# Side matmuls of an attention loop placed in three groups per step instead of one

## The reference, cut to what matters

```python
p = split_in(h @ w_in)                    # one projection feeds everything below
y_a = mlstm_branch(...)                   # "ml":  mLSTM, then @ ml_w_o
y_b = mla_branch(...)                     # "mla": 8 heads, softmax attention, then @ mla_w_o
y_c = natten_branch(...)                  # "na":  8 heads, windowed attention with bias, then @ na_w_o
# attend: s = q @ k^T * scale; p = softmax(s); o = p @ v
y = (sigmoid(g_a) * y_a + sigmoid(g_b) * y_b + sigmoid(g_c) * y_c) @ w_out
```

## Time and profile before

| | |
|---|---|
| median of 3 runs | 2104.02 us (2099.68 to 2108.57) |
| the profiled execution | 2104.02 us, of which the span is 2102.2 us |
| mean granted TensorE clock | 0.903 |
| PE busy | 1733.3 us, 82% of the span |
| DVE, ACT, POOL busy | 51%, 35%, 30% |
| first S to last S of the loops na0, mla0, na1, mla1 (starts) | 388.9 to 507.6; 634.0 to 751.7; 1573.9 to 1643.5; 1737.9 to 1806.0 |

### The profile page before, as it was taken

How to read it: one execution, slowest core, us unless ns; L and a number is a source line. 1 busy time by engine, 2 the same in 40 slices (tenths; PEclk the granted TensorE clock), 3 DMA queues, 4 the chain that set the end, 5 groups by cost and what they waited for, 6 DMA issues and landing times.

```text
span 2102.2 us, 24715 instructions
## 1 busy us (share of the span) xinstructions
PE 1733.3 (82%) x9538; PEld 1456.1 (69%) x9538; DVE 1069.2 (51%) x1895; ACT 729.7 (35%) x1354; POOL 627.1 (30%) x380
## 2 busy tenths in 40 slices
PE   2594768999769998888989897676599869878998
PEld 1483548877457777656868686465598748778998
DVE  6786953143173335156746454426325265555555
ACT  3223324343333423242313131433334344435443
POOL 0441114222122212243535442430331311233443
PEclk9697879999779999988999998798899979998999
DMA  7342212211111123213443333220222202343553
GB/s 273 122 184 100 100 31 76 63 63 42 46 40 52 46 101 110 100 51 128 170 152 140 149 131 140 100 86 0 71 79 62 95 28 91 132 170 102 184 187 130
DMA packets 55846, 216.98 MB, mean 103 GB/s; under 512 B 17313, under 2 KB 17459, under 8 KB 41139
## 3 DMA queue, kind: packets, MB, share of 16 engines
q1 hardware_dynamic: 41232, 202.13, 27.2%
q10 hardware_dynamic: 14499, 13.29, 2.0%
HBM read 210.15 MB, written 5.24 MB: 102 GB/s over the span
## 4 chain that ended last, share of the span: by engine, by line
PE 66%; DVE 17%; ACT 5%; issue 4%; POOL 3%; DMA 3%; ACTq 1%; POOLq 0%; SPq 0%; DVEq 0%
PE bank L1494 35%; PE bank L1536 8%; PE bank L1508 6%; PE bank L1656 3%; PE bank L1769 3%; PE bank L1748 3%; PE bank L1518 2%; DVE mjunk L1002 2%; DVE acc L1002 2%; DVE arena L1028 2%; ACT wH L642 2%; POOL wL L511 2%; PE bank L1755 1%; DMA raw<-in_p_ff 1%; POOL wL L513 1%
## 5 line engine op out<-in xcount | busy, mean ns | idle before, releaser
L642 ACT ACTIVATE wH<-raw 128x1280 fp32r<-128x1280 f32 (+5 forms) x380 | 295.3, 833 | 661.3 <-PE bank L1494 410.2
L513 POOL TENSOR_TENSOR wL<-raw,wH 128x768 fp32r<-128x768 f32 (+5 forms) x190 | 325.4, 1717 | 477.7 <-ACT wH L642 460.4
L511 POOL TENSOR_TENSOR wL<-raw,wH 128x1280 fp32r<-128x1280 f32 (+5 forms) x98 | 231.3, 2360 | 682.4 <-ACT wH L642 682.4
L1494 PE MATMUL bank<-hH,wH 128*128 128x512 f32 (+1 forms) x976 | 349.6, 358 | 81.2 <-POOL hL L530 50.1
L1494 PE MATMUL bank<-hL,wH 128*128 128x512 f32 (+1 forms) x976 | 342.5, 351 | 0.0
L1494 PE MATMUL bank<-hH,wL 128*128 128x512 f32 (+1 forms) x976 | 342.1, 350 | 0.0
L1494 PEld LDWEIGHTS bank<-hH,wH 128*128 128x128 f32 x976 | 193.1, 198 | 121.1 <-issue 54.7
L1494 PE MATMUL bank<-oH,wH 128*128 128x512 f32 (+1 forms) x576 | 198.3, 344 | 35.8 <-POOL wL L513 35.8
L1494 PEld LDWEIGHTS bank<-hH,wL 128*128 128x128 f32 x976 | 193.7, 198 | 22.0
L1494 PEld LDWEIGHTS bank<-hL,wH 128*128 128x128 f32 x976 | 194.4, 199 | 20.2
L1494 PE MATMUL bank<-oL,wH 128*128 128x512 f32 (+1 forms) x576 | 196.9, 342 | 0.0
(11 more groups left out here) (204 smaller groups left out, 3133.0 us busy)
## 6 DMA issues: line engine op xcount, KB each, us to landing
raw<-in_p_ff SPq DMA_DIRECT2D x64, 1024.0 KB, 4.9
acc<-in_p_mod SPq DMA_DIRECT2D x48, 1024.0 KB, 5.0
raw<-in_p_ml SPq DMA_DIRECT2D x12, 1024.0 KB, 7.5
raw<-in_p_na SPq DMA_DIRECT2D x12, 1024.0 KB, 4.8
raw<-in_p_mga SPq DMA_DIRECT2D x16, 512.0 KB, 3.5
raw<-in_p_mgc SPq DMA_DIRECT2D x16, 512.0 KB, 3.5
raw<-in_p_mgb SPq DMA_DIRECT2D x8, 1024.0 KB, 4.8
raw<-in_p_out SPq DMA_DIRECT2D x8, 1024.0 KB, 4.8
```

What stands on the lines that cost most here:

```text
L511: pool.tensor_tensor(l_[:, 0:cut], r_[:, 0:cut], h_[:, 0:cut].bitcast(F32), ALU.subtract)
L513: pool.tensor_tensor(l_[:, cut:k * w], r_[:, cut:k * w], h_[:, cut:k * w].bitcast(F32), ALU.subtract)\
L642: act.activation(flat(wH, n)[:, part], flat(raw, n)[:, part], ACT.Copy)\
L1494: ins = pe.matmul(dst, w_[:, kk, c:c + P], r_[:, kk, lo:TOK], start=kk == k0 and m == 0, stop=kk == k0 + kn - 1 and m == 2)
```

## The change

The `pace` side matmuls of a step are issued in three groups: a third behind S, a third behind T, and the rest behind V. Their number per step is the same, and so is their order among themselves; ACT, DVE and SP have the same instructions in the same order.

```diff
@@ the loop over steps, tensor block
                             pe.matmul(bank[4 + step % 2][:, 0:nk], q_, k_, start=True, stop=True).then_inc(S(tag + "s").up(1), 1)
+                            pump(pace // 3)
                         if 0 <= step - 1 < len(items):
...
                             ins.then_inc(S(tag + "pt").up(1), 1)
+                        if step < len(items):
+                            pump(pace // 3)
                         if 0 <= step - 2 < len(items):
...
                             ins.then_inc(S(tag + "o").up(1), 1)
                         if step < len(items):
-                            pump(pace)
+                            pump(pace - 2 * (pace // 3))
```

## The result

| | before | changed |
|---|---|---|
| median, same chip | 2101.91 us (4 runs, 2099.68 to 2108.57) | 2135.17 us (4 runs, 2132.34 to 2138.35) |
| profiled execution, span | 2104.02, 2102.2 | 2135.12, 2133.3 |
| granted clock, whole run | 0.903 | 0.900 |

The ratio is 1.0153, with an interval of 1.0125 to 1.0182: slower by 1.5%. I had forecast 2130, in a range of 2110 to 2146.

What follows compares the result with a forecast made beforehand. PE bounds layer 0; in layer 1 an exp-to-exp ring through three engines does. Layer 1 +27.4, layer 0 -4.0 and loop ends +2.1 give +25.5 us on 2104.02: 2129.5, told as 2130, range 2110 to 2146.

Steps and rivals of the forecast that it cites:

- The ring in layer 1: Exp-to-exp cycle through PE, ACT and DVE in na1 and mla1: a pair 9.10 to 11.30 us in na1, +27.4 us.
- the gate wait: Layer 1, even steps: first gate matmul waits for the previous chunk's tanh, 1.57 us after the odd exp, delaying T and V.
- the wait for bank 3: Layer 1, between T and V: the branch chunk's first matmul waits; 5.65 us to next exp, below 5.95.
- the other half: Layer 1, even exp to odd exp through ACT's and DVE's weight work: stays 5.95 us, getting no late PE work.
- Layer 0: Loops of na0 and mla0: -4.0 us from V's wait after O, +2.1 us at the loops' ends.
- The oL wait: Layer 0, V waiting for oL after O: disappears as V stands 1.39 us further behind O, -2.0 us per loop.
- The loop ends: End of each layer 0 loop: last T waits for the exp, 1.05 us later, twice, +2.1 us.
- PE's restart: Switching between side matmuls and T or V on PE: taken as 0, with 5 us kept for the range.
- Rival D: Each group of side matmuls costs PE a restart, up to +23 us: 2135 to 2152; chance 0.06.
- Rival A: Finer filling helps: layer 1's T finds its exp done, ring wait goes, -8.5 us in all, 2095.5; chance 0.08.
- Rival B: Layer 1's wait for the tanh is met; only six side matmuls between T and V count: +8 us, 2112; chance 0.12.
- Rival C: PE's clock falls in layer 1's gappy loops: 35 us in all pairs, 17 in half of them, 2147; chance 0.12.

Runs made afterwards that it cites:

- layer 1 alone: Three groups of side matmuls in layer 1 only, layer 0 as in the kernel before: 2138.98 against 2103.25 us, ratio 1.0159.
- the early tanh: Three groups in layer 1 only, with the tanh that frees bank 2 moved ahead of the odd step's exp: 2122.34 against 2103.25 us, ratio 1.0090.
- the S group alone: Kernel before, but in layer 1 six side matmuls behind S, none behind T, twelve behind V: 2120.93 against 2103.25 us, ratio 1.0086.
- layer 0 alone: Three groups of side matmuls in layer 0 only, layer 1 as in the kernel before: 2107.70 against 2103.25 us, ratio 1.0016.
- the three groups without sharing: Three groups in layer 1, with layer 1's low halves of side weights all made by POOL, none by DVE: 2117.32 us, one execution.
- the first run of the group behind S: Kernel before, but six side matmuls behind S only in the step after O: 2100.22 against 2102.76 us, ratio 0.9985; run again, 0.9978.

## Why the prediction was right

**The ring in layer 1, +27.4 us told.** The mechanism held. The clean comparison is layer 1 alone, whose loops of na1 and mla1 began at the clock of before: they are 13.4 and 13.5 us longer, 27.0 together. From the exp of item 2 to that of item 14 na1 went from 56.15 to 68.53 us, +12.4 where 13.2 - 0.7 = 12.5 was told; up to the exp of item 2 +1.5 (1.5 told), behind that of item 14 -0.4 (-0.3 told). That the stages of the changed kernel add up to 27.35 is in part luck: its loops are 10.9 and 14.4 us longer, 25.2 together, because na1's began at a higher clock, and mla1's projection, where nothing was moved, adds 2.0. Of the links, the gate wait is shown by the early tanh, which gives back 1.24 us of a pair in na1 before the wait for bank 3 takes over, the six matmuls behind T by the difference to the S group alone (0.72), and the other half, unchanged at 5.95, by the chain. Only the gate wait ahead of T was shorter than the "about 1.2 us" told, 0.98. Both extremes were tried apart: with the group behind S only the ring was 4.63, behind T only 4.19, as the sum of the remaining links says.

**Layer 0, -1.9 us told.** The oL wait went, -2.0 a loop. The loop ends cost 1.1 and 1.6 us instead of 1.05 each, and 0.4 us a loop of longer steps came on top, a term that I had set to nothing; by the run with layer 0 alone the sum is -0.4 by the loops and about 0 by the stages. Most of the -2.0 in the changed kernel's profile, which looks like a hit, is luck with the clock: against layer 0 alone, with the same order in these loops, its loop of na0 is 1.4 us shorter at its first steps and its projection of mla0 1.4 us. The terms that were mis-sized are these two small ones, the loop end of mla0 and the longer steps, together over 1 us.

**PE's restart, 0 told with 5 us in the range.** 0.01 to 0.02 us a step in layer 0; the odd steps of the three groups without sharing take 4.33 us where one group took 4.34 to 4.35, so layer 1 shows none. Rival D falls.

**Rival A** (finer filling helps) falls with all six kernels that put a group into every step of layer 1: each was slower, two of them by a single execution. The interleaving that I weighed as a rule (the Trainium skill, Perfetto Trace Analysis, Optimization Strategy) did not pay in these loops. Where filling meets a real wait, as behind O, it does help: the loops of layer 0 are 2.15 us shorter, and the ratios are 0.9985 and 0.9978. **Rival B** (the gate wait is met) falls by the waits for 809, six in na1's loop and six in mla1's, and by the S group's run. **Rival C** (the clock falls in the loops) falls by the windows: 1.00 and 0.97.

**What the forecast missed.** 2135.17 is 5 us above 2130, but the two medians differ by 33.3 us, the profiles by 31.1, the terms told by 25.5. The sum started from 2104.02 us, 2.1 above the median that the result was then compared with. In the profiles the four loops account for 23.3 us and 7.8 lie where no instruction was moved: 3.2 in the middle, 3.1 in the tail, 2.0 in the projections and -0.6 in the head. In the tail it is the clock, 0.94 instead of 0.96. Ten microseconds at its start, before and after:

```profile
1817.16:1827.16 10.00, 9.32 (x75) 9.15 (x76) 2.51 (x2) 3.59 (x6) 1.73 (x1) 1.00 0.56 210
```

```profile
1845.15:1855.15 10.00, 10.00 (x66) 10.00 (x67) 0.50 (x1) 1.88 (x2) 0.00 (x0) 0.77 0.57 210
```

Every kernel whose layer 1 loops changed their length has a longer tail, +1.2 to +3.1 us. Of those that kept it, layer 0 alone had -0.2 and the first run of the group behind S -0.1, but the repeat of the latter had +3.2 with the same program, and its first ten microseconds were at 1.00. So the same program gives both, and whether the +3.1 belongs to the change stays open. The middle's +3.2 lies within what it does anyway: over the fourteen profiles it takes 730.2 to 737.2 us with identical instructions, the changed kernel's being the longest.

## What to carry to other kernels

Before work is put into a gap of an in-order queue, ask what its first instruction waits for and who stands behind it: filler with a wait of its own, placed inside a ring through other engines, makes that wait everybody's. Find the ring first (the spacing of one repeated instruction, here the exp, odd and even apart), and put filler only where the queue waits longer than the filler's own release takes: six matmuls in the step after O gained, six in every step of layer 1 lost. When one wait is taken off, read the chain again, since another may stand right behind it. Then look at the stages behind the one that was sped up, since work moved to another engine there took back all that the loops had gained.

## What the hardware did that I had not expected

- DVE stood still for a POOL instruction: 1.45 us for an operation of 0.29 that reads two SBUF operands, while one with a PSUM operand was not disturbed.
- The loop of na0, about 1 us shorter by the six matmuls behind S in the steps after O, was followed by a granted clock of 0.83 instead of 0.75 in mla0's projection, which took 109.1 to 109.2 us instead of 114.9, in all four profiles with that edit. The other nine changed profiles have 113.5 to 115.3 us there, and in two of them na0's loop was shorter still (by 1.5 and 1.9 us), so the length alone does not decide it; what does stays open. A small edit can shift the clock of the stage behind it by more than it gains itself.
- Stretches that nothing touches vary from profile to profile: the head of the kernel by 302.7 to 308.3 us, the middle by 730.2 to 737.2. The kernel before ran between 2096.6 and 2111.1 us, and gains of 2 us needed about ten executions on either side. Differences of 1 to 4 us between two single profiles, outside the loops, can be of this kind.
